# One tile of a depthwise convolution on TensorE, split into even and odd columns

## What is computed

```python
def conformer_conv_branch(h, w_in, b_in, conv_w, conv_b, norm_g, norm_b, w_out, b_out):
    proj = h @ w_in + b_in
    val, glu_gate, z = jnp.split(proj, 3, axis=-1)
    u = val * jax.nn.sigmoid(glu_gate)
    u = lax.conv_general_dilated(
        u, conv_w[:, None, :], window_strides=(1,), padding=[(CONV_KERNEL - 1, 0)],
        dimension_numbers=('NWC', 'WIO', 'NWC'), feature_group_count=CONV_WIDTH) + conv_b
    u = jax.nn.silu(layer_norm(u, norm_g, norm_b))
    u = u * jax.nn.silu(z)
    return u @ w_out + b_out
```

## Time and profile before

| | us |
|---|---|
| median of 3 runs | 822.82 |
| lowest, highest | 822.71, 824.22 |
| the profiled execution | 821.95 |
| its span, first to last instruction | 820.0 |

### The profile page before, as it was taken

How to read it: one execution, slowest core, us unless ns; L and a number is a source line. 1 busy time by engine, 2 the same in 40 slices (tenths; PEclk the granted TensorE clock), 3 DMA queues, 4 the chain that set the end, 5 groups by cost and what they waited for, 6 DMA issues and landing times.

```text
span 820.0 us, 11442 instructions
## 1 busy us (share of the span) xinstructions
PE 807.9 (99%) x3891; PEld 681.8 (83%) x3891; DVE 604.8 (74%) x1026; ACT 395.7 (48%) x711; POOL 543.0 (66%) x335
## 2 busy tenths in 40 slices
PE   8999999999999999999999999999999999999996
PEld 7888888888888887888898788888888888888885
DVE  2699999999999978994833192038778888887217
ACT  4654444455564368622342444256566665655210
POOL 4677999896999954594354438426867776387530
PEclk9999999999999999999999999999999999999999
DMA  6333332330032324444233335215666664663412
GB/s 220 103 103 103 86 93 85 95 104 26 23 106 85 108 80 145 158 159 129 52 109 114 98 103 166 57 41 175 199 191 203 198 203 123 193 203 130 154 52 102
DMA packets 123019, 100.01 MB, mean 122 GB/s; under 512 B 15354, under 2 KB 107616, under 8 KB 122972
## 3 DMA queue, kind: packets, MB, share of 16 engines
q1 hardware_dynamic: 122972, 99.42, 40.1%
HBM read 82.36 MB, written 12.58 MB: 116 GB/s over the span
## 4 chain that ended last, share of the span: by engine, by line
PE 92%; DMA 3%; POOL 1%; ACT 1%; DVE 1%; SPq 1%; issue 1%; DVEq 0%
PE bank L1692 89%; DMA x_in<-in_x_dram 1%; DMA prob_kept<-prob 1%; PE bank L1997 1%; PE bank L1998 1%; DMA prob_moved<-prob_kept 0%; ACT bank L1201 0%; POOL bundle_lo L855 0%; PE bank L1871 0%; POOL pt_lo L886 0%; SPq L626 0%; ACT bundle_hi L1135 0%; PE bank L1990 0%; DMA qr_swap<-qr_raw 0%; PE bank L1924 0%
## 5 line engine op out<-in xcount | busy, mean ns | idle before, releaser
L730 POOL TENSOR_TENSOR w_lo<-w_raw,w_hi 128x1024 fp32r<-128x1024 f32 x102 | 252.7, 2486 | 114.4 <-ACT w_hi L927 106.8
L1328 DVE SCALAR_TENSOR_TENSOR bank<-u,conv_w,bank 128x512 f32<-128x512 f32 x357 | 238.9, 758 | 0.5
L1692 PE MATMUL bank<-xt_hi,w_lo 128*128 128x512 f32 (+1 forms) x392 | 152.0, 388 | 0.0
L927 ACT ACTIVATE w_hi<-w_raw 128x1024 fp32r<-128x1024 f32 x102 | 106.3, 1054 | 92.6 <-PE bank L1692 29.3
L1692 PE MATMUL bank<-xt_hi,w_hi 128*128 128x512 f32 (+1 forms) x392 | 150.9, 385 | 0.0
L1692 PE MATMUL bank<-xt_lo,w_hi 128*128 128x512 f32 (+1 forms) x392 | 150.8, 385 | 0.0
L1692 PEld LDWEIGHTS bank<-xt_lo,w_hi 128*128 128x128 f32 x392 | 73.7, 188 | 15.0 <-issue 0.5
L1692 PEld LDWEIGHTS bank<-xt_hi,w_hi 128*128 128x128 f32 x392 | 73.6, 188 | 14.9
L1692 PEld LDWEIGHTS bank<-xt_hi,w_lo 128*128 128x128 f32 x392 | 73.7, 188 | 14.9 <-issue 0.5
L767 POOL TENSOR_TENSOR acc<-acc,tap_product 128x512 f32<-128x512 f32 x60 | 77.8, 1297 | 9.7 <-ACT tap_product L960 4.5
L1692 PE MATMUL bank<-ht_hi,w_lo 128*128 128x512 f32 (+1 forms) x208 | 76.4, 367 | 0.0
(11 more groups left out here) (213 smaller groups left out, 1725.6 us busy)
## 6 DMA issues: line engine op xcount, KB each, us to landing
w_raw<-in_a_w_in_dram SPq DMA_DIRECT2D x48, 512.0 KB, 3.7
w_raw<-in_b_w_in_dram SPq DMA_DIRECT2D x20, 512.0 KB, 3.5
prob_kept<-prob SPq DMA_DIRECT2D x16, 640.0 KB, 3.2
prob_moved<-prob_kept SPq DMA_DIRECT2D x64, 160.0 KB, 3.2
w_raw<-in_a_w_out_dram SPq DMA_DIRECT2D x16, 512.0 KB, 4.0
w_raw<-in_b_w_out_dram SPq DMA_DIRECT2D x16, 512.0 KB, 3.5
bundle_raw<-in_b_w_uq_dram SPq DMA_DIRECT2D x16, 256.0 KB, 4.4
x_in<-in_x_dram SPq DMA_DIRECT2D x4, 512.0 KB, 5.9
```

Source lines behind the costliest of these rows:

```text
L730: nc.gpsimd.tensor_tensor(w_lo[slot][:], w_raw[raw][:], w_hi[slot][:].bitcast(F32), ALU.subtract).then_inc(w_lo_ready, 1)
L927: nc.scalar.activation(w_hi[slot][:], w_raw[raw][:], ACT.Copy).then_inc(w_hi_ready, 1)
L1328: nc.vector.scalar_tensor_tensor(out=inner[:] if k < TAPS - 1 else acc[:, t, :], in0=u[:, t, k:k + SEQ], scalar=conv_w[:, column:column + ...
L1692: last = nc.tensor.matmul(out_ap, a, b, start=(start and n == 0 and m == 0), stop=(stop and n == len(parts) - 1 and m == 2))
```

## The change

Tile 13 is convolved in phases. Its 512 columns are taken apart into even and odd ones, and a block of 64 channels with both phases fills the 128 partitions. Taps become 128 x 128 matrices of four 64 x 64 diagonals, one for each pair of an input and an output phase: 16 offsets to a block, two blocks, 32 matrices, whose products are 256 columns wide. Before: 31 x 3 products of 512 columns; now 32 x 3 of 256. Tile 12 takes 28 taps as matrices rather than 21, so that DVE has 3 left rather than 10, and the groups of slots are 7, 7, 7, 7 and 4 wide rather than 5, 5, 5, 6 and 10.

What this needs: `phase_taps`, taps placed by partition and phase, cleared by POOL, filled by four small transfers (SP, behind the load of column 7) and split by ACT and POOL; `phases_hi` and `phases_lo`, the input by phases, for which half of each goes over to the other 64 partitions by four transfers between z1's load and z2's; and the result, of which half comes out on the wrong partitions: ACT copies it to `sums_far`, two transfers (SP, between the loads of z5 and z6) bring it to `sums_moved`, and ACT adds the bias in `keep_far_sums`, behind its split of z4 and ahead of its first `keep_z`. Each matrix of tile 13 is written by ACT in two instructions of 64 columns.

```diff
-        MATRIX_TAPS = (21, TAPS)
-        TAP_GROUPS = tuple(range(a, b) for a, b in zip((0, 5, 10, 15, 21), (5, 10, 15, 21, 31)))
+        MATRIX_TAPS = (28, TAPS)
+        TAP_GROUPS = tuple(range(a, b) for a, b in zip((0, 7, 14, 21, 28), (7, 14, 21, 28, MATRICES)))
+        KEPT_PARTS = 1 + 4
...
+            for i in range(2):
+                load_z(i)
+            sp.wait_ge(phases_hi_ready, 3)
+            for part in range(2):
+                sp.dma_start(phases_hi[far[part], part, 0:PHASE_COLS].bitcast(F32), odd_hi[near[part], :].bitcast(F32)
+                             ).then_inc(phases_landed, 16)
...
+            for i in range(2, 6):
+                load_z(i)
+            sp.wait_ge(far_sums_ready, 2)
+            for part in range(2):
+                sp.dma_start(sums_moved[near[part], :], sums_far[far[part], :]).then_inc(far_sums_landed, 16)
+            for i in range(6, 2 * ROUND):
+                load_z(i)
...
+            def phase_strips_lo(g):
+                if g < SHARED_SLOTS:
+                    act.wait_ge(diag_used, g + 1)
...
+                for slot, part, d in phase_matrices(g):
+                    for b in range(PHASES):
+                        nc.scalar.activation(
+                            diag_lo[:, slot, b * HALF_P:(b + 1) * HALF_P], ident_both[:], ACT.Copy,
+                            scale=phase_taps_lo[:, part, 2 * d + b:2 * d + b + 1].bitcast(F32)).then_inc(diag_lo_ready, 1)
...
+            def keep_far_sums():
+                act.wait_ge(far_sums_landed, 32)
+                for part in range(2):
+                    nc.scalar.activation(out_phase(part, part), sums_moved[near[part], :], ACT.Identity,
+                                         bias=conv_bias(near[part])).then_inc(pe_conv_kept, 1)
...
                 if i == 2:
-                    keep_conv(1)
+                    keep_near_sums()
+                if i == 4:
+                    keep_far_sums()
                 if i >= 4:
                     keep_z(i - 4)
...
+                for g in PHASE_ORDER:
+                    pe.wait_ge(diag_hi_ready, diag_hi_value(1, g))
+                    pe.wait_ge(diag_lo_ready, diag_lo_value(1, g))
+                    for slot, part, d in phase_matrices(g):
+                        last = product(bank[MATRIX_BANK[1]][:, part * OUT_COLS:(part + 1) * OUT_COLS],
+                                       [(diag_hi[:, slot, :], diag_lo[:, slot, :], phases_hi[:, part, d:d + OUT_COLS],
+                                         phases_lo[:, part, d:d + OUT_COLS])], d == 0, d == OFFSETS - 1)
```

More of the change, by code:

```diff
@@ L782, in conv_matrices, with phase_strips @@
                                         ALU.mult).then_inc(diag_hi_ready, 1)
-            def conv_input_lo(m):
[L785 to L788, removed]
+            def phase_strips(g):
+                if g < SHARED_SLOTS:
+                    pool.wait_ge(diag_used, g + 1)
+                else:
+                    pool.wait_ge(phase_taps_hi_ready, 1)
+                    nc.gpsimd.tensor_tensor(phase_taps_lo[:], phase_taps[:], phase_taps_hi[:].bitcast(F32), ALU.subtract
+                                            ).then_inc(phase_taps_lo_ready, 1)
+                for slot, part, d, n in phase_runs(g):
+                    taps = phase_taps_hi[:, part, 2 * d:2 * (d + n)].bitcast(F32)
+                    nc.gpsimd.tensor_tensor(diag_hi[:, slot:slot + n, :].rearrange("p n (b c) -> p (n b) c", b=PHASES),
+                                            ident_both[:].unsqueeze(1).broadcast_to([P, 2 * n, HALF_P]),
+                                            taps.unsqueeze(2).broadcast_to([P, 2 * n, HALF_P]),
+                                            ALU.mult).then_inc(diag_hi_ready, 1)
@@ L973, in conv_input_hi, with split_phase_taps @@
+            def split_phase_taps():
+                act.wait_ge(phase_taps_landed, 64)
+                nc.scalar.activation(phase_taps_hi[:], phase_taps[:], ACT.Copy).then_inc(phase_taps_hi_ready, 1)
             def conv_input_hi(m):
                 act.wait_ge(u_ready, MATRIX_TILES[m] + 1)
[L975 to L981, removed]
-                                     bias=vec[:, V_CONVB + t:V_CONVB + t + 1]).then_inc(pe_conv_kept, 1)
+                tile = u[:, MATRIX_TILES[m], :]
+                if m == 0:
+                    nc.scalar.activation(cu_hi[:], tile, ACT.Copy).then_inc(cu_hi_ready, 1)
+                    return
+                nc.scalar.activation(odd_hi[:], phase_of(tile, 1), ACT.Copy).then_inc(phases_hi_ready, 1)
+                for part in range(2):
+                    nc.scalar.activation(phases_hi[near[part], part, 0:PHASE_COLS],
+                                         phase_of(u[near[part], MATRIX_TILES[1], :], 0), ACT.Copy
+                                         ).then_inc(phases_hi_ready, 1)
@@ new lines, in keep_first_conv, with out_phase, conv_bias @@
+            def keep_first_conv():
+                t = MATRIX_TILES[0]
+                act.wait_ge(diag_used, SHARED_SLOTS)
+                nc.scalar.activation(bank[MATRIX_BANK[0]][:], bank[MATRIX_BANK[0]][:], ACT.Identity,
+                                     bias=vec[:, V_CONVB + t:V_CONVB + t + 1]).then_inc(pe_conv_kept, 1)
+            def out_phase(part, b):
+                return phase_of(acc[near[part], MATRIX_TILES[1], :], b)
+            def conv_bias(rows):
+                t = MATRIX_TILES[1]
+                return vec[rows, V_CONVB + t:V_CONVB + t + 1]
@@ new lines, in keep_near_sums @@
+            def keep_near_sums():
+                act.wait_ge(pe_conv_done, 1)
+                sums = [bank[MATRIX_BANK[1]][:, part * OUT_COLS:(part + 1) * OUT_COLS] for part in range(2)]
+                for part in range(2):
+                    nc.scalar.activation(sums_far[far[part], :], sums[part][far[part]], ACT.Copy).then_inc(far_sums_ready, 1)
+                for part in range(2):
+                    nc.scalar.activation(out_phase(part, 1 - part), sums[part][near[part]], ACT.Identity,
+                                         bias=conv_bias(near[part])).then_inc(pe_conv_kept, 1)
@@ L1788, in _ @@
                 value_gate(j)
[L1789 to L1790 removed]
+            convolve_first()
+            convolve_phases()
             def spread_rstd():
```

147 lines of the change are left out of this document (114 added, 33 removed).

## The result

The changed kernel took 829.24 us, median of 4 runs (828.51 to 831.28); the kernel before, beside it, 822.77 (4 runs, 820.37 to 824.22). The ratio is 1.0089, with a 95% interval of 1.0071 to 1.0107: slower by 0.9%. The forecast was 828.5. The profiled execution took 831.28 with a span of 829.5 us; the spans of the other three were 827.2, 827.7 and 826.7, so it is the longest of them, and the size of the loss is better read stage by stage than from its span.

What follows compares the result with a forecast made beforehand. PE, busy 99% of the span, bounds the kernel, with DVE and POOL nearly level. Span 820.0 + 5.7 for the later mean = 825.7, plus 1.95 to device time and 0.87 to the median: 828.5 us, range 824.5 to 832.5.

Steps and rivals of the forecast that it cites:

- PE's saving: In PE's convolution: 31.08 us instead of 36.32, so PE is ready for z0 5.24 us earlier.
- ACT and POOL behind the fourth group: Before z1: later slot release and 14 short ACT steps shift POOL's split by 6.55 us; PE waits 5.6 us.
- The far sums: At z4: ACT is held by the transfers into `sums_moved`, landing at 243.5, so POOL loses another 2.7 us.
- The mean: At the mean: POOL's last addition 9.25 us later, DVE waits 9.4 us, the mean comes 5.7 us late.
- PE's second wait: Ahead of the mean: PE arrives at 289, the mean comes at 293.2, so PE waits some 4 us.
- what PE loses after the first is swallowed by the second: In the clock rival: PE's loss after the 5.6 us wait before z1 disappears in the wait at the mean.
- the short one for the bank of z0: At z4, which writes z0's bank: PE waits from 245.5 to 246.3, which disappears in the waits around it.
- likeliest case: Whole kernel: the mean 5.7 us late, nothing changed after it, 828.5 us, at 58%.
- the rival with + 2.0 us: Behind the mean: PE's clock falls in the wait and about 9 products lose 0.227 us each, 830.5 us; 13%.
- The sum: Whole kernel: span 820.0 + 5.7 = 825.7 us, giving 828.5 us for the median.
- The hidden transfer: Rival at z4: the far sums' transfer costs nothing, only the late group counts, 3.0 us, 825.8 us; 17%.
- DVE sets the mean: Rival at the mean: POOL is not late, the mean comes 3.7 us earlier with DVE, 819.1 us; 6%.

Runs made afterwards that it cites:

- the 21-tap kernel: The changed kernel with tile 12 back to 21 taps as matrices, groups 5, 5, 5, 6 and 11, phases of tile 13 kept: 825.82 us, ratio 1.0057 to before.
- spread and far sums: The changed kernel with shared taps spread (2 ahead, then 2, 2, 2, 4 behind the groups) and the far sums' copy at z6: 819.08 us, ratio 0.9950 to before.
- spread alone: The changed kernel with shared taps 2 ahead of the first group and 2, 2, 2, 4 behind the four, not 1, 1, 1, 9: 823.04 us, ratio 1.0019.
- far sums at z6: The changed kernel with ACT's copy of `sums_moved` moved from z4 to z6, nothing else: 824.90 us, ratio 1.0042 to before.

## Why the prediction was right, point by point

**PE's saving, right.** 30.97 us for the convolution against 31.08 forecast, products of 256 columns at 0.12.

**ACT and POOL behind the fourth group, right.** From the start of the convolution ACT began the group at 19.72 (forecast 19.74) and reached the shared tap at 23.08, 6.45 us later than before (forecast 6.55, bounds 5.9 to 7.3). A step of 64 columns took (210.82 - 207.46) / 14 = 0.24 us; the estimate from the slope was 0.246. POOL's 11 additions took 15.64 us as before, and z1 was ready 6.36 us later. The wait ahead of z1 was 5.35 us, forecast 5.6.

**The far sums, right, a little too small.** Both transfers were in 4.5 us after POOL had let SP go on, forecast 4.3 (243.5 - 239.22). POOL lost 3.19 us, and 3.15 by the experiment that moved it, against 2.7: each of the two copies took 0.525 us, not the 0.40 taken from a mean of other shapes, and the load of the table and the silu came behind them as the chain said. What the 21-tap kernel adds is that the landing isn't a constant: behind the same load it took 5.8 us in the one execution profiled there, and POOL lost 4.47, inside my upper bound of 5.6. The Trainium skill, "DMA: Bandwidth & Descriptors", section "Queues, rings and completion order", says that a queue's descriptors are taken in the order of the ring on each engine. The traces agree with that: from issue to landing, the two transfers of 64 KB behind a load of 512 KB took 3.3 to 3.5 us each, once 4.6, where 2.0 was the median of such a size before.

**The mean, right.** POOL 9.46 us late (forecast 9.25), DVE waiting 9.52 (forecast 9.4), DVE's own end 95.23 after the start of the convolution (forecast 282.2 - 187.05 = 95.15), the mean 5.94 late (forecast 5.7).

**PE's second wait: there, but shorter.** 3.09 us, forecast 4. I had PE arrive at 289; it arrived at 291, since its products behind z1 had run at 1.2 GHz for 13 steps and lost 2.7 us. The step "what PE loses after the first is swallowed by the second" is what happened. Between z1 and the mean PE has no other wait, so the short one for the bank of z0 didn't come.

**The clock behind the mean: the wrong side of a right alternative.** The forecast's likeliest case had nothing behind the mean, and the rival with + 2.0 us stood at 13%. The clock fell, in both profiled executions of the changed kernel and in two experiments that had a wait of 4 us there, and cost 1.4, 2.9, 1.4 and 2.8 us: on average 2.1, which is the rival's price. What failed is first its chance: the likeliest case put this term at nothing. The price itself was met by luck. It came from a low level of 3.9 us, and no fall had that; the level lasted about 3.4 us or about 6.8, so that a fall cost 1.4 or 2.8 to 2.9, and never 2.0. I had a row for it, the fall behind the last product of the program, and it lay level with the wait of about 4 us that I forecast; that spoke for the fall at least as much as against it, and I read it as against. One row was also too little to read a time from: ahead of the nine falls of these runs PE had stood still for 2.0 to 5.2 us. The Trainium skill, "TensorE: Matmul & The Clock Gate", section "Why this matters for your kernels", warned against idle gaps between bursts of products; the runs here agree with it, with nine falls in nine waits of 2.97 us and more, and I had weighed it too low.

**The sum.** Mean + 5.9 and clock + 1.4 to 2.9 make 7.3 to 8.8 us on the span; the medians differ by 829.24 - 822.77 = 6.5 on the one chip and 829.59 - 821.56 = 8.0 on the other. The forecast's own sum was + 5.7. That 829.24 is only 0.7 from 828.5 is luck in part: the sum left out the clock's 1.4 to 2.9 us, and it began from a kernel before that came out at 822.8 in its first runs; against the 821.6 and 822.0 of the later ones, the clock's 2 us are needed. By mechanism the rival "the clock falls" is the case that occurred, with all of the likeliest case's steps inside it.

**The other rivals.** The hidden transfer fell: it cost 3.15 us. "DVE sets the mean" was not what this kernel did, but named what was to be had, and the point from which it decides, 3.56 us of delay on POOL, held on both sides: with a last addition 0.8 us earlier than before (spread and far sums) DVE set the mean; with one 2.4 later (spread alone), less than 3.56, the mean still came 1.1 earlier than before.

## What to carry to other kernels

When several engines run level, price a change on the queue that feeds them all, not on the one it relieves: 5.35 us saved on TensorE turned into waits because the slots' release, fourteen short instructions and one copy placed behind a transfer made GpSimd 9.5 us late. Where two engines serve each other in order, put a step that needs a transfer a column or two behind the transfer, and look for gaps ahead of and between groups before stacking work behind the last: those two moves added no work and turned 1.0089 into 0.9950. And count a wait of TensorE twice, once for itself and once for the products that run at 1.2 GHz after it; a wait in front of other waits can hide that price, one in front of a chain can't.

## What the runs showed of the hardware that I had not expected

- Waits of 2.97 to 5.35 us of TensorE were each followed by a fall of the granted clock from 1.00 to 0.50 (nine of them, in all the runs that had such a wait); waits of 1.02 and 1.71 us ahead of the same product, and one of 0.37, weren't. The fall had no fixed place in the wait: it came between 2.0 us (21 taps, ahead of z1) and 5.2 us (far sums at z6, ahead of z1) after PE's last product, read from the granted clock in stretches of a quarter of a microsecond. Product steps of 512 columns were 0.427 us at 1.2 GHz and 0.227 at 2.4.
- The low level reached far into the work that followed: about 3.4 us in one execution of the changed kernel, about 6.8 in another, with waits of 2.97 and 3.09 us. All nine falls had one of these two lengths, about 3.4 us three times and about 6.8 six times, and the length of the wait didn't decide which (4.03 us: 3.4; 4.07 us: 6.8). Why the same kernel does the one or the other stays open.
- Two transfers of 64 KB behind a load in the same queue were in 4.5 to 4.6 us after the queue could go on in four executions, and 5.8 in a fifth, with the same load ahead of them. What lengthened it wasn't tried.
- Fifteen products that compute nothing of use made the kernel faster, by 1.4 to 2.9 us in the stretch behind the mean and by 3.1 in the medians.
